# Two of 22 more K-tile pairs of the output matmuls by seven products, and the first weights of the input stage loaded in another order

## The reference, cut to what matters

```python
h = rms_norm(x, ffn_pre_g)
gate, up = split(h @ w_ffn_in, 2)            # 256 x 2048 by 2048 x (2 * 5632)
x = x + rms_norm((silu(gate) * up) @ w_ffn_out, ffn_post_g)    # 256 x 5632 by 5632 x 2048
```

## Time and profile before

| | |
|---|---|
| median of 3 runs | 2393.44 us (2393.33 to 2393.86) |
| the profiled execution | 2393.11 us |
| its span | 2391.3 us |
| busy in the span | PE 2369.4 us (99%), DVE 1850.9 us (77%), ACT 1399.4 us (59%) |
| granted TensorE clock | 0.999 |
| DMA | 485.23 MB, mean 203 GB/s |

### The profile page before, as it was taken

The page is one execution under the profiler, slowest core; times in us unless marked ns, Lnnn a source line. Parts: engine busy times, 40 slices in busy tenths (PEclk is TensorE's granted clock), DMA queues, the critical chain, the costliest instruction groups (busy, mean ns, idle before and its releaser), DMA issues.

```text
span 2391.3 us, 34797 instructions
## 1 busy us (share of the span) xinstructions
PE 2369.4 (99%) x12027; PEld 1977.7 (83%) x12027; DVE 1850.9 (77%) x2572; ACT 1399.4 (59%) x1939; POOL 195.2 (8%) x252
## 2 busy tenths in 40 slices
PE   9999999999999999999999999999999999999998
PEld 7888888887888888888887888998788888888887
DVE  5568878677899999987667536767799999997766
ACT  5665457656666666655445445655666666664444
POOL 1000000000111111210000000000021111111000
PEclk9999999999999999999999999999999999999999
DMA  7775544555878788866566775444798887867655
GB/s 233 243 217 176 167 151 163 166 186 176 267 206 247 212 224 232 221 200 218 189 213 200 216 228 167 132 134 136 235 229 244 210 247 206 233 177 243 216 180 176
DMA packets 249217, 485.23 MB, mean 203 GB/s; under 512 B 19770, under 2 KB 22074, under 8 KB 248592
## 3 DMA queue, kind: packets, MB, share of 16 engines
q1 hardware_dynamic: 216768, 410.51, 52.5%
q0 software_dynamic: 31760, 72.16, 15.0%
q10 hardware_dynamic: 576, 1.05, 0.1%
HBM read 474.21 MB, written 9.44 MB: 202 GB/s over the span
## 4 chain that ended last, share of the span: by engine, by line
PE 93%; DVE 3%; ACT 2%; issue 1%; DMA 0%; ACTq 0%; SPq 0%; DVEq 0%
PE g L1456 11%; PE g L1457 11%; PE g L1458 11%; PE g L362 5%; PE g L364 5%; PE g L363 5%; PE g L1965 4%; PE g L1967 4%; PE g L1966 4%; PE m L1293 3%; PE m L1295 3%; PE m L1294 3%; PE g L1293 2%; PE g L1295 2%; PE g L1294 2%; PE g L2902 1%
## 5 line engine op out<-in xcount | busy, mean ns | idle before, releaser
L350 DVE TENSOR_TENSOR wl<-raw,wh 128x1024 fp32r<-128x1024 f32 (+1 forms) x500 | 601.4, 1216 | 331.9 <-ACT wh L346 325.1
L346 ACT ACTIVATE wh<-raw 128x1024 fp32r<-128x1024 f32 (+1 forms) x499 | 519.0, 1052 | 465.3 <-PE g L364 128.3
L1456 PE MATMUL g<-wh,act_hi 128*128 128x512 f32 x640 | 250.4, 391 | 2.3 <-DVE wl L1384 2.3
L1457 PE MATMUL g<-wl,act_hi 128*128 128x512 f32 x640 | 249.1, 389 | 0.0
L1458 PE MATMUL g<-wh,act_lo 128*128 128x512 f32 x640 | 249.1, 389 | 0.0
L1232 ACT ACTIVATE wh<-in_x 128x1024 fp32r<-128x1024 f32 (+1 forms) x160 | 152.8, 955 | 108.4 <-PE g L1458 71.3
L1456 PE MATMUL g<-wh,ht_hi 128*128 128x512 f32 x544 | 211.8, 389 | 0.0
L1458 PE MATMUL g<-wh,ht_lo 128*128 128x512 f32 x544 | 211.7, 389 | 0.0
L1457 PE MATMUL g<-wl,ht_hi 128*128 128x512 f32 x544 | 211.6, 389 | 0.0
L1384 DVE TENSOR_TENSOR wl<-raw,wh 128x1024 fp32r<-128x1024 f32 x160 | 195.5, 1222 | 13.7 <-ACT wh L1379 3.4
L362 PE MATMUL g<-wh,act_hi 128*128 128x512 f32 x512 | 203.2, 397 | 0.9 <-DVE wl L350 0.4
(11 more groups left out here) (546 smaller groups left out, 5114.8 us busy)
## 6 DMA issues: line engine op xcount, KB each, us to landing
raw<-in_w_in SPq DMA_DIRECT2D x111, 512.0 KB, 4.5
raw<-in_w_ffn_in SPq DMA_DIRECT2D x106, 512.0 KB, 4.7
raw<-in_ffn_w_in SPq DMA_DIRECT2D x106, 512.0 KB, 4.8
raw<-in_w_ffn_out SPq DMA_DIRECT2D x88, 512.0 KB, 5.2
raw<-in_ffn_w_out SPq DMA_DIRECT2D x88, 512.0 KB, 5.1
raw<-in_nsa_w_in SPq DMA_DIRECT2D x80, 512.0 KB, 4.3
raw<-in_w_out SPq DMA_DIRECT2D x32, 512.0 KB, 4.3
raw<-in_nsa_w_out SPq DMA_DIRECT2D x32, 512.0 KB, 4.3
```

The costliest lines, as they stand in the source:

```text
L346: nc.scalar.activation(wh[:, j % SLOTS, 0:n], raw[:, j % SLOTS, 0:n], ACT.Copy).then_inc(hi_done, 1)
L350: nc.vector.tensor_tensor(wl[:, j % SLOTS, 0:n], raw[:, j % SLOTS, 0:n], wh[:, j % SLOTS, 0:n].bitcast(F32), ALU.subtract).then_inc(lo_don ...
L1456: nc.tensor.matmul(dst, h, whk, start=(t in starts and k == 0), stop=False)
L1457: nc.tensor.matmul(dst, h, wlk, start=False, stop=False)
```

## The change

- `FO_K` goes from 4 to 6: S0 to S5 in each half of each output stage. The list has 112 places, it had 104. The gaps were 10, 5, 5, 7 units ahead of S0 to S3 in the first half, and are now 8, 3, 3, 4, 3, 3; in the second half (behind the 9 and now 8 units that end the first) 6, 6, 7, 7 become 5, 4, 4, 5, 3, 2. The first block starts at place 8, it started at 10.
- The sums of rows are made at places 5, 12 and 27, they were made at 6 and 15.
- The first of the four sums goes into a quarter of `ht_hi` and `ht_lo` that no product reads any more; so `fo_hi` and `fo_lo` hold three sums for each pair, and the split is an instruction of 256 and one of 768 columns in place of one of 1024.
- In `fo1` one part of `fo_lo` lies in the space of x, so the eight loads that bring x back start only when the last block has been multiplied, and VectorE waits for them at the last place of the list.
- In the input stages' opening the loads of the loop's first round are issued in another order; ScalarE makes its row sums one place later; one memset (L1705) goes, and the sum at L1731 becomes a copy there.

The core of the diff:

```diff
-FO_K = 4
-FO_GAPS = ((10, 0), (5, 0), (1, 4), (1, 6), (1, 8)), ((6, 0), (6, 0), (4, 3), (1, 6), (1, 9))
-FO_SUMS_AT = (6, 15)
+FO_K = 6
+FO_GAPS = (((8, 0), (3, 0), (3, 0), (1, 3), (0, 3), (0, 3), (1, 7)),
+           ((5, 0), (4, 0), (3, 1), (3, 2), (0, 3), (0, 2), (1, 8)))
+FO_SUMS_AT = (5, 12, 27)
...
         def pool_bring_x(pool, name, out_name):
             pool.wait_ge(x_moved, x_moved_no(name, 1))
+            u0 = SLOTS + gemms[out_name]["u0"]
+            last = OUT_AT[2 * FO_K - 1]
+            if out_name == "fo1":
+                pool.wait_ge(unit_used, u0 + last + 4)
             for n in range(8):
-                pool.wait_ge(lo_done, SLOTS + gemms[out_name]["u0"] + 4 + 2 * n)
+                pool.wait_ge(lo_done, u0 + (last + 4 + n if out_name == "fo1" else 4 + 2 * n))
...
-            for b in range(2):
-                block_a(1, b)
-                block_b(1, b)
-            for n in range(SLOTS):
+            def old_done(n):
                 sp.wait_ge(lo_done, SLOTS + s["u0"] + FF_FIRST - SLOTS + n + 1)
-                unit(1, n)
+
+            block_a(1, 0)
+            old_done(0)
+            unit(1, 0)
+            block_a(1, 1)
+            block_b(1, 0)
             sp.wait_ge(ss_done, SS[turn] + 2)
             sp.wait_ge(x_moved, x_moved_no(name, 1))
-            for b in range(2, SEVENS):
-                block_a(1, b)
+            block_a(1, 2)
+            old_done(1)
+            unit(1, 1)
+            block_a(1, 3)
+            old_done(2)
+            unit(1, 2)
+            old_done(3)
+            unit(1, 3)
+            for b in range(1, SEVENS):
                 block_b(1, b)
...
                 if n - 2 in FO_SUMS_AT:
-                    b = FO_SUMS_AT.index(n - 2) + 1
-                    k = slice(2 * (b - 1), 2 * b)
-                    dve_sums_lo(dve, fo_sums[:, :, :, :], fo_hi[:, k, :, :], fo_lo[:, k, :, :], summed_no(name, b) + 1)
-                    dve.wait_ge(ff_summed, summed_no(name, b + 1))
-                if n == OUT_AT[FO_K - 1] + 7:
+                    r = FO_SUMS_AT.index(n - 2)
+                    dve.wait_ge(ff_summed, summed_no(name, r + 1) + 2)
+                    nc.vector.tensor_tensor(first_sums(ht_lo, 4 * r), fo_sums[:, :, 0, :], first_sums(ht_hi, 4 * r).bitcast(F32), ALU.subtract)
+                    dve_sums_lo(dve, fo_sums[:, :, 1:4, :], fo_hi[r][:, :, :, :], fo_lo[name][r][:, :, :, :], summed_no(name, r + 1) + 1)
+                    dve.wait_ge(ff_summed, summed_no(name, r + 2))
+                if n == (len(OUT) - 1 if name == "fo1" else OUT_AT[FO_K - 1] + 7):
                     dve.wait_ge(x_moved, x_moved_no({"fo1": "ff1", "fo2": "ff2"}[name], 2))
...
-                    if j == 14:
-                        link_d(dve, nc.vector.memset(shared[:, 0:T, :], 0.0))
                 dve.wait_ge(unit_used, SLOTS + s["u0"] + 8)
                 dve.wait_ge(ff_summed, ff_summed_no(name, 6))
-                gate_rows(0)
+                nc.vector.tensor_copy(ff_b[0][:, :, :], g[:, 0:T, :]).then_inc(pair_free[0], 1)
```

More of the change, by code:

```diff
@@ L168, in build @@
         fo_sums = at("fo_sums", [P, 2, 4, P], o_al + 4096)
-        fo_hi = at("fo_hi", [P, FO_K, 4, P], o_ah, F32R)
-        fo_lo = at("fo_lo", [P, FO_K, 4, P], o_ah + 8192, F32R)
+        fo_hi = [at(f"fo_hi{r}", [P, 2, 3, P], o_ah + (0, 3072, 12288)[r], F32R) for r in range(FO_K // 2)]
+        fo_lo01 = [at(f"fo_lo{r}", [P, 2, 3, P], o_ah + 6144 + 3072 * r, F32R) for r in range(2)]
+        fo_lo = {"fo1": fo_lo01 + [at("fo_lo2", [P, 2, 3, P], o_x + 12288, F32R)],
+                 "fo2": fo_lo01 + [at("fo_lo3", [P, 2, 3, P], o_gb + 4096, F32R)]}
         fo_kept = {"fo1": at("fo_kept1", [P, T, NB], o_ga + 4096), "fo2": at("fo_kept2", [P, T, NB], o_gb)}
@@ L1200, in dve_sums_lo, with first_sums, fo_block_sums @@
             nc.vector.tensor_tensor(lo, sums, hi.bitcast(F32), ALU.subtract).then_inc(ff_summed, 1)
-        def first_sums(buf, r):
-            k0 = 2 * SEVEN_K + 4 * r
+        def first_sums(buf, k0):
             return buf[:, k0:k0 + 4:2, P:2 * P]
+        def fo_block_sums(name, b):
+            return lambda n: ((fo_hi[b // 2][:, b % 2, n - 1, :], fo_lo[name][b // 2][:, b % 2, n - 1, :]) if n else
+                              (ht_hi[:, 2 * b, P:2 * P], ht_lo[:, 2 * b, P:2 * P]))
         def block_sums(b):
@@ L1500, in pe_out @@
                         pe.wait_ge(ff_summed, summed_no(name, 2 + b // 2))
[L1501 removed]
+                    pe_seven(pe, cyc, n, ht_hi, ht_lo, 2 * b, fo_block_sums(name, b),
                              b == 0, b == FO_K - 1, s["pair0"][1] + c + 1)
@@ L1515, in act_out @@
                 if n - 2 in FO_SUMS_AT:
-                    b = FO_SUMS_AT.index(n - 2) + 1
-                    act_sums_hi(act, fo_sums[:, :, :, :], fo_hi[:, 2 * (b - 1):2 * b, :, :], summed_no(name, b) + 1)
+                    r = FO_SUMS_AT.index(n - 2)
+                    act.wait_ge(ff_summed, summed_no(name, r + 1) + 1)
+                    nc.scalar.activation(first_sums(ht_hi, 4 * r), fo_sums[:, :, 0, :], ACT.Copy)
+                    act_sums_hi(act, fo_sums[:, :, 1:4, :], fo_hi[r][:, :, :, :], summed_no(name, r + 1) + 1)
                 if n - SLOTS in OUT_AT and OUT[n - SLOTS][2] == FO_K - 1:
@@ L1658, in opening @@
                     act_lead_in(act, turn, j)
-                    if j in (10, 13):
-                        r = j // 13
+                    if j in (11, 14):
+                        r = j // 14
                         act_sums_hi(act, sums[r][:, :, 1:4, :], sums_hi[:, 2 * r:2 * r + 2, :, :], ff_summed_no(name, 3 * r + 1))
@@ L1665, in opening @@
                 for r in range(2):
-                    ins = nc.scalar.activation(first_sums(act_hi, r), sums[r][:, :, 0, :], ACT.Copy)
+                    ins = nc.scalar.activation(first_sums(act_hi, 2 * SEVEN_K + 4 * r), sums[r][:, :, 0, :], ACT.Copy)
                 ins.then_inc(ff_summed, 1)
@@ L1703, in opening @@
                         dve_sums_lo(dve, sums[r][:, :, 1:4, :], sums_hi[:, k, :, :], sums_lo[:, k, :, :], ff_summed_no(name, 3 * r + 1))
-                    if j == 14:
-                        link_d(dve, nc.vector.memset(shared[:, 0:T, :], 0.0))
                 dve.wait_ge(unit_used, SLOTS + s["u0"] + 8)
                 dve.wait_ge(ff_summed, ff_summed_no(name, 6))
-                gate_rows(0)
+                nc.vector.tensor_copy(ff_b[0][:, :, :], g[:, 0:T, :]).then_inc(pair_free[0], 1)
                 dve.wait_ge(ff_summed, ff_summed_no(name, 7))
                 for r in range(2):
-                    ins = nc.vector.tensor_tensor(first_sums(act_lo, r), sums[r][:, :, 0, :], first_sums(act_hi, r).bitcast(F32), ALU.subtract)
+                    ins = nc.vector.tensor_tensor(first_sums(act_lo, 2 * SEVEN_K + 4 * r), sums[r][:, :, 0, :], first_sums(act_hi, 2 * SEVEN_K + 4 * r).bitcast(F32), ALU.subtract)
                 ins.then_inc(ff_summed, 1)
```

2 lines of the change are left out of this document (1 added, 1 removed).

## The result

The changed kernel takes **2414.39 us** (median of 4 runs, 2409.91 to 2416.18), the kernel before 2393.65 (4 runs, 2393.33 to 2394.03): ratio 1.0082, interval 1.0070 to 1.0094. It is slower by 0.8%. The sign and the mechanism were forecast; the size was not: +10.9 was said, +20.7 came. The time lies at the very end of the range: its upper bound was 2414, and the median is 0.4 above that. The profiled execution took 2415.27 us with a span of 2413.5, 22.2 more than the span before.

What follows compares the result with a forecast made beforehand. The prediction took PE to bound the kernel. Its terms -5.4 - 2.4 + 18.7 = +10.9 us, against the profiled execution of 2393.11, gave 2404 us, with 2388 to 2414 for 8 in 10.

Steps and rivals of the forecast that it cites:

- Matmuls saved: Output stages: two more blocks in two halves of two stages save 24 matmuls at 0.227 us each, -5.4 us.
- The loops' first wait: Start of the input stages' loops: DVE comes about 1.6 us earlier, two PE waits shrink; -2.4 us, ends 0 and -2.65.
- Rival 4: Input stages: the wait at the loops' start stays, from ScalarE's table load or the loop's entry; 2406, chance 0.05.
- What the short gaps cost: Output stages: PE waits at blocks behind short gaps, 8.6 us a stage plus 1.5 in fo2, together +18.7 (5 to 30).
- The rule: Output stages: at each block with a gap of 3, PE waits L - 4.8 us; L taken as 6.0, so 1.2.
- fo2's loads of x: fo2, S0 to S2: two or three 256 KB loads of x fall in a gap, 0.9 us each; +1.5 us added.
- With gaps of 4 and more there are 2.7 us and more to spare: Output stages: blocks behind gaps of 4 or more have at least 2.7 us of room for q1's load.
- L: Landing time of the load of q1, a block's second load; ends 3.8 and 7.0 us, 6.0 taken.
- x in fo1: End of fo1: the eight late loads of x land in time, cost 0, with some 0.4 us of cover.
- Rival 1: Output stages: loads land in time, only DVE's own waits of 4.4 us stay; 2390, down to 2386; chance 0.26.
- Rival 2: Output stages: loads bunch once PE waits, landings go to 7.0 us, 28 us of waits in all; 2414; chance 0.14.
- The Trainium skill's fit: GpSimd-issued loads: 2.0 us + bytes / 436 GB/s, 3.2 us for 512 KB, so no gap of 3 would wait.

Runs made afterwards that it cites:

- the kernel with small loads: Changed kernel with all of SP's weight loads in the output stages from the fifth unit on cut to 64 KB (result not the reference's): 2388.03 us, ratio 0.9977.
- the run with the loads alone: Kernel before with only the order of the loads in the input stages' opening changed, DVE and ScalarE as before: 2393.54 us, one run.
- the kernel with gaps of 4: Changed kernel, same six blocks, gaps 8, 4, 4, 4, 3, 3 and 5, 4, 4, 4, 4, 4, sums of rows at 5, 13, 29: 2411.31 us, one run.
- the kernel with the late gain: Changed kernel with GpSimd's 1 MB load of the last norm's gain held until the end of fo2's first half: 2411.84 us, ratio 1.0075.
- the kernel with the small q1 load: Changed kernel with only q1's load in both output stages cut from 512 KB to 64 KB (result not the reference's): 2404.15 us, ratio 1.0045.

## Why the prediction was right, and where it was too small

**Matmuls saved, -5.4.** 12003 for 12027; the kernel with small loads shows the gain: its span of 2386.0 is 2391.3 - 5.4 - 3.0 + 2.5 of waits, + 0.4 behind them, + 0.6 of half clock at the border, which makes 2386.4.

**The loops' first wait, -2.4.** It was about 3.0: both waits went entirely, and the rest of the sum was right in its reason (DVE was late), as the run with the loads alone shows. Rival 4 is refuted.

**What the short gaps cost, +18.7.** The rule was right and the terms too small. By blocks, forecast and measured in fo1 and fo2:

| block | forecast | fo1 | fo2 |
|---|---|---|---|
| S1, with the sums of rows | 1.6 | 0.50 + 0.73 | 0.49 + 0.74 |
| S2 | 1.2 | 1.49 | 1.09 + 4.07 |
| S3 | 1.6 | 0.56 + 0.74 | 0 |
| S4 | 1.2 | 1.33 | 0.66 |
| S5 | 1.2 | 0.95 | 3.01 |
| second half, S2 and S3 | 0 | 0.47 + 0.75 | 0 |
| second half, S4 and S5 | 0.3 + 1.5 | 0 + 2.45 | 0.92 + 1.59 |
| last units | 0 | 0 | 0.87 |
| fo2's loads of x | +1.5 | | |

For fo1 the sum was 8.6 against 10.0: good. For fo2 it was 10.1 against 13.4, and one step failed, "in fo2 the loads of x ... I add 1.5". I counted the loads that the diff moves, and not the one that stands behind them in GpSimd's program: 1 MB, four loads of x in size. Issued 1.4 us ahead of q1's, it took S2 from 2.7 us (the run that moves it away) to 5.2. The diff doesn't touch it; the shorter list of units ahead moved it into a gap of 3.

"With gaps of 4 and more there are 2.7 us and more to spare" is wrong too: fo1's second half waits 0.47 and 0.75 behind gaps of 4 and 5, fo1's S3 waits behind a gap of 4 for loads and not for the sums of rows (it doesn't with small loads), and the kernel with gaps of 4 has more. I let PE come later by a unit and left q1's load where it was. At those two blocks of fo1 it went out 5.4 and 9.3 us after the start of the block ahead (at a gap of 3: 4.0 to 4.1), since the `wl` that frees its slot is a later one and itself waited for a plain load; with all loads small the second figure is 6.2. The rest of the chain is as said: these times, L and 4.18 us for DVE give waits of 0.5 and 0.9, for the 0.47 and 0.75 seen.

**What no step priced: about 6.5 us behind the waits.** A PE that has waited doesn't go on at 0.227 us at once. After each wait of more than 0.4 us at a block or a unit the first interval is 0.31 to 0.34, and after some of the long ones the clock is at half: 0.43 us from start to start, granted clock 0.50 over 2212 to 2217, then 1.00 again. I had put a wait at its own length. It may also be why four runs of the changed kernel spread over 6 us (13 of the kernel before over 4); that wasn't tested.

**x in fo1, 0.** Right, and with as little cover as said: the kernel with gaps of 4 uses it up.

**Rivals.** Rival 1 (loads land in time) is wrong: L was over 4.8 at every block of the table of landings. Rival 2 (the queue gives way) had the mechanism that makes up the difference, and its 2414 is what came; it put the excess on an L of 7.0 everywhere, though, and what came is 5.4 to 6.2 at most blocks, 8.0 and 10.1 at two, and the half clock. That the median came to its 2414 doesn't make it right.

What makes the 8.0 at S5 of fo2 stays open. None of GpSimd's loads is beside it, and SP issues the load behind the same three others, at the same distances, as at S5 of fo1 (5.8). In its last 1.7 us hardly anything moves (columns as in the earlier trace rows), and the load lands 2.7 us behind the one ahead, 1.3 at S5 of fo1:

```profile
2254.00:2256.00 2.00, 2.00 (x10) 1.67 (x10) 0.14 (x1) 0.37 (x2) 0.00 (x0) 1.00 0.15 56
```

It isn't a freak of one execution: in the kernel with the late gain the same load took 7.7.

**Page against row.** The Trainium skill's fit for a load by itself, cited in the prediction, gives no wait at gaps of 3. The runs side with the rows: a 64 KB load took 4.9, 5.8 and 9.0 us behind others at the blocks above, and 1.9 among small ones.

## What to carry to other kernels

Matmuls saved pay only as long as the loads that feed them keep their distance; here 24 matmuls of 0.227 us were bought with gaps that put each critical load close behind three others, and 21 us of waits came back. Price a load by the queue that it is issued into, every issuer's, untouched loads that now fall there included, and shrink one load in a run to see whether it is its size or its place that matters. And a change made of independent parts should be timed part by part: the opening alone wins 3 us, which the whole hides. A unit more in a gap isn't a whole unit's time more for the load, if the load waits for that unit's conversion.

## What was not expected of the hardware

**Half clock behind short waits, but not each time.** PE's granted clock fell to 0.50, that is 1.2 GHz in place of 2.4, after waits of 2.45 us (7 starts 0.43 apart) and 4.07 (12 starts). After the wait of 3.01 at S5 of fo2 it did not, as this row and the start of its follower show:

```profile
2259.79 0.50 PE L1162 MATMUL m<-wh,ht_hi 128*128 128x512 f32 x1 [2.85 <-DVE wl L1140]
2260.13 0.40 PE L1163 MATMUL m<-wl,ht_hi 128*128 128x512 f32 x1
```

Nor did it after 3.07 us in the kernel with the small q1 load or after 2.64 in the one with gaps of 4, while 2.85 at S5 of fo2 with the late gain had it. So the 2.3 us that I named in an expectation is no threshold. At the border behind fo1, with the same wait of 1.44 us, it fell in the changed kernel and not in the one before, and the kernel before with one gap of 3 has it too:

```profile
1282.00:1284.00 2.00, 2.00 (x7) 1.58 (x7) 0.97 (x3) 0.61 (x2) 0.00 (x0) 0.50 0.68 244
```

So the waits of 1.4 to 4.1 us in these traces had a price of 0 to 2.5 us on top of their length, and a single profile doesn't tell which. The Trainium skill, "TensorE: Matmul & The Clock Gate", section "Part 1: The HAM clock gate (the "warmup" mystery)", says of a kernel's first matmuls that how many run at the lower clock varies from run to run for one kernel. The 0, 7 and 12 here stand behind different waits in mid-kernel and one execution, so no run here shows that.

**An eighth of the bytes, and a landing that another load sets.** 64 KB in 4.9, 5.8 and 9.0 us behind loads of 512 KB and beside one of 1 MB, in 1.8 us where the load ahead landed 1.1 us after this one was issued, and in 1.9 us among its like; at 20 of 24 blocks within 0.25 us of the load ahead.
